# Issuing the page loads of both caches from GpSimd's queue instead of SyncE's, in a two-layer hybrid decoder step

## The reference

```python
# 8 decode sequences, 512 past positions in 4 pages of 128; page_table (8, 4) int32
k_past = cache_k[page_table, j].reshape(bs, n_pages * PAGE_SIZE, DIFF_HEADS, DIFF_HEAD_DIM)
v_past = cache_v[page_table, j].reshape(bs, n_pages * PAGE_SIZE, DIFF_HEADS, DIFF_HEAD_DIM)
...
a = probs(qf[..., :DIFF_HALF], k1) - lam * probs(qf[..., DIFF_HALF:], k2)   # softmax(q k * scale + bias)
o = jnp.einsum('bhqk,bkhd->bqhd', a, vf)
...
mixed = jnp.concatenate([y_pool, o.reshape(B, T, DIFF_WIDTH)], axis=-1)     # pooling groups beside the heads
return mixed @ w_out
```

## Time and profile before

| | |
|---|---|
| Time, median of 3 runs | 1458.28 us (1456.0 to 1458.72) |
| The profiled execution, its own time | 1461.25 us |
| Its span | 1459.5 us, mean granted TensorE clock 0.984 |
| PE busy (matmul) | 1392.3 us, 95% |
| DVE, ACT, POOL busy | 47%, 34%, 25% |
| DMA | 140.92 MB, queue q1 busy for 27.4% of 16 engines' span |
| Page loads | 32 of cache_k and 32 of cache_v, 256 KB each, all by SP |

### The profile page before, as it was taken

The page is one execution under the profiler, slowest core; times in us unless marked ns, Lnnn a source line. Parts: engine busy times, 40 slices in busy tenths (PEclk is TensorE's granted clock), DMA queues, the critical chain, the costliest instruction groups (busy, mean ns, idle before and its releaser), DMA issues.

```text
span 1459.5 us, 28313 instructions
## 1 busy us (share of the span) xinstructions
PE 1392.3 (95%) x11816; PEld 1171.8 (80%) x11816; DVE 685.7 (47%) x979; ACT 499.6 (34%) x711; POOL 371.9 (25%) x465
## 2 busy tenths in 40 slices
PE   8999899999999999899999999998799999999997
PEld 6866588888888888687788788787688888888886
DVE  4556453333333323676676676776443333333222
ACT  5334343322223322334334334334244223223221
POOL 1004312212212001354344344344121212221000
PEclk9999799999999999899999999999999999999999
DMA  6566423422233221100120120120222232233211
GB/s 225 208 215 205 139 87 109 150 97 104 86 125 120 80 108 57 58 30 30 60 86 30 60 86 30 59 88 15 95 94 88 87 115 86 97 115 119 99 61 59
DMA packets 32045, 140.92 MB, mean 97 GB/s; under 512 B 4537, under 2 KB 6841, under 8 KB 20058
## 3 DMA queue, kind: packets, MB, share of 16 engines
q1 hardware_dynamic: 31962, 139.75, 27.4%
HBM read 128.63 MB, written 11.11 MB: 96 GB/s over the span
## 4 chain that ended last, share of the span: by engine, by line
PE 84%; DVE 10%; issue 3%; SPq 1%; DMA 1%; ACT 1%; POOL 0%; DVEq 0%; ACTq 0%; POOLq 0%
PE P L1591 59%; PE P L1963 8%; PE P L1954 7%; DVE arena L1360 2%; PE P L1969 2%; DVE arena L1401 1%; PE P L2151 1%; DVE arena L1515 1%; PE P L2128 1%; PE P L2118 1%; PE P L1805 1%; SPq L338 1%; PE P L2089 1%; PE P L1938 1%; DVE arena L1336 1%
## 5 line engine op out<-in xcount | busy, mean ns | idle before, releaser
L1591 PE MATMUL P<-zh,wh 128*128 128x260 f16 x1728 | 332.8, 274 | 2.3 <-DVE wl L1093 2.1
L1591 PE MATMUL P<-zl,wh 128*128 128x260 f16 x1728 | 332.8, 274 | 0.0
L1591 PE MATMUL P<-zh,wl 128*128 128x260 f16 x1728 | 332.8, 274 | 0.0
L1073 DVE SCALAR_TENSOR_TENSOR wl<-stage,wh 128x2048 f16<-128x2048 f32 (+1 forms) x76 | 187.3, 2465 | 210.2 <-ACT wh L702 196.0
L1591 PE MATMUL P<-arena,wh 128*128 128x260 f16 x1832 | 280.4, 275 | 3.3 <-DVE arena L1336 2.8
L1591 PEld LDWEIGHTS P<-arena,wh 128*128 128x128 f16 x1832 | 178.0, 97 | 32.5 <-issue 4.2
L1591 PEld LDWEIGHTS P<-zh,wh 128*128 128x128 f16 x1728 | 165.8, 97 | 35.1 <-issue 6.5
L1591 PEld LDWEIGHTS P<-zh,wl 128*128 128x128 f16 x1728 | 167.4, 97 | 26.5
L1591 PEld LDWEIGHTS P<-zl,wh 128*128 128x128 f16 x1728 | 167.2, 97 | 26.2
L1591 PE MATMUL P<-arena,wl 128*128 128x260 f16 x916 | 176.9, 274 | 0.0
L702 ACT ACTIVATE wh<-stage 128x2048 f16<-128x2048 f32 (+1 forms) x82 | 165.6, 2020 | 2.8 <-PE P L1954 2.8
(11 more groups left out here) (324 smaller groups left out, 1578.5 us busy)
## 6 DMA issues: line engine op xcount, KB each, us to landing
stage<-w_gu SPq DMA_DIRECT2D x44, 1024.0 KB, 4.8
stage<-w_in SPq DMA_DIRECT2D x23, 1024.0 KB, 4.9
stage<-w_dn SPq DMA_DIRECT2D x16, 1408.0 KB, 5.8
arena<-cache_k SPq DMA_DIRECT2D x32, 256.0 KB, 3.6
stage<-w_out SPq DMA_DIRECT2D x8, 1024.0 KB, 5.1
arena<-cache_v SPq DMA_DIRECT2D x32, 256.0 KB, 3.0
arena<-delta_state SPq DMA_DIRECT2D x8, 512.0 KB, 3.6
o_ds<-arena SPq DMA_DIRECT2D x8, 512.0 KB, 6.7
```

The source lines that it names most:

```text
L1073: nc.vector.scalar_tensor_tensor(out=wl[:, j, 0:words], in0=stage[:, j, 0:words], scalar=WS, in1=wh[:, j, 0:words], op0=MUL, op1=SUB).then ...
L1591: mm = nc.tensor.matmul(pm[j][:, c, :], w[:, wslot, o:o + 128], x[:, k, c * CH:(c + 1) * CH], start=(k == first and w is wh and x is xh), ...
```

## The change

`load_kv` is moved from SP's program to POOL's, with its waits. Nothing is changed in what a load reads or writes, in the number of slots, or in the program of PE, DVE and ACT. In POOL's program the loads get these places: 0 to 2 before the clearing of `qpad` and `apad`, 3 to 10 behind it and ahead of pooling group 0, 11 and 12 behind group 0, and 13 to 15 behind group 1. SP keeps the weights, the bias and the outputs.

```diff
@@ SP: every load_kv call goes, and the function with them
-            load_kv(0)
             project_in(3)
 ...
-            load_kv(1)
             sp.wait_ge(strip_out, 16)
 ...
-            load_kv(2)
             for u in range(4, 8):
                 project_in(u)
-            for n in range(3, 7):
-                load_kv(n)
             project_mix(0)
-            for n in range(7, 11):
-                load_kv(n)
             sp.wait_ge(pm_free, 12)
 ...
             project_mix(1)
-            for n in range(11, 2 * NDEC):
-                load_kv(n)
             sp.wait_ge(dext, 4)
@@ POOL
+            def load_kv(n):
+
+                src, b, s = (cache_k, n, n % NKV) if n < NDEC else (cache_v, n - NDEC, n % NKV)
+                if n >= NKV:
+                    pool.wait_ge(kv_used, n - NKV + 1)
+                for g in range(NPG):
+                    i = b * NPG + g
+                    page = pool.value_load(pt[0:1, i:i + 1], min_val=0, max_val=cache_k.shape[0] - 1)
+                    nc.gpsimd.dma_start(kv[:, s, g, :], src[bass.ds(page, 1)].rearrange("a p n -> (a p) n")
+                                 ).then_inc(kv_in[s], 16)
+
+            pool.wait_ge(c_in, 16 * 7)
+            for n in range(NKV):
+                load_kv(n)
             pool.wait_ge(strip_out, 16)
-            pool.wait_ge(c_in, 16 * 7)
             link(nc.gpsimd.memset(qpad, 0.0))
 ...
             pool.nop().then_inc(consts, 1)
+
+            for n in range(NKV, NDEC + NKV):
+                load_kv(n)
 
             for i, g in enumerate(GROUPS):
 ...
                 nc.gpsimd.tensor_tensor(dT[:, SEQ:T], dT[:, SEQ:T], ext[:, g, :, 15], SUB).then_inc(d_ready, 1)
+                for n in ((11, 12), (13, 14, 15), (), ())[i]:
+                    load_kv(n)
```

More of the change, by code:

```diff
@@ L329, in stream @@
                         weights(src, base + 2 * i + j, j, bass.ds(2 * i + j, 1), words)
[L331 to L340, removed]
             def project_in(u):
```

## The result

| | before | after |
|---|---|---|
| Median (5 runs each) | 1458.28 us (1454.53 to 1459.28) | 1467.18 us (1465.13 to 1469.0) |
| Ratio, 95% interval | | 1.0067 [1.005, 1.0085] |
| The profiled execution, its own time | 1461.25 us | 1466.75 us |
| Its span, mean granted clock | 1459.5 us, 0.984 | 1465.1 us, 0.984 |

The forecast was 1468.4. So the traces say where the time went, and the medians how much it is.

A forecast was written before the change was run, and what follows sets the result against it. PE's weight products, untouched, were taken as the bound (59% of the chain). POOL's line releases the fourth projection at 160.9 + 16p = 181.4 against 171.25, 10.1 us later: 1458.3 + 10.1 = 1468.4 us, range 1460 to 1486.

The forecast's parts named there:

- p = 1.28: Assumed cost in us of one page load on POOL, halfway between 1.10 and 1.45.
- The one line on POOL: Loads 12 to 15 and groups 1 to 3 run in order on POOL, delaying PE's fourth pooling projection by 10.1 us.
- The page: Issuing a page on POOL costs 1.28 us, register work plus DMA instruction, with ends of 0.96 and 2.05.
- DVE beside POOL: Delaying group 0 loosens its collision with DVE; up to 2.5 and some 2 us back, counted as nothing.
- Load 3: On POOL it no longer stands behind SP's eighth weight unit, so PE's full 1.1 us wait is won.
- PE's stalls: PE waits for cache_v at three products, then for POOL at the third and fourth projection, inside the 10.1 us.
- The dear page: Rival, chance 0.27: POOL's DMA instruction costs 0.8 to 1.3 us and POOL bounds the mixer; 25 us late at p = 1.75.
- the second ceiling: POOL's 52 pages and four groups from 76.3 us end at 105.2 + 52p, binding only above p = 1.55.
- Loads in time: Rival, chance 0.09: POOL issues loads 13 to 15 by 157 us, PE doesn't stop; about 10 us faster, 1448.
- The cheap page: Rival, chance 0.09: register work overlaps the DMA before it, a page is 0.76 us or less; no change, 1456 to 1461.
- The rules of the Trainium skill: POOL's DMAs land some 0.4 us later (1468.8); DVE locking POOL out of descriptor writing adds 2 us (1470.4).
- I add no clock cost: Behind the fourth projection PE ran at the low clock in before too, so no clock term was added.

The follow-up runs named there:

- e1: The changed kernel with loads 13 to 15 moved ahead of pooling group 1 on POOL: 1467.29 us, 1.0057 of before.
- e2: The changed kernel with loads 13 to 15 back on SP, loads 0 to 12 staying on POOL: 1454.07 us, 0.9965 of before.
- e3: The changed kernel with loads 11 to 15 back on SP, loads 0 to 10 staying on POOL: 1453.91 us, 0.9968 of before.
- e8: The kernel before with only loads 11 to 15 moved to POOL, loads 0 to 10 staying on SP: 1469.93 us, 1.009 of before.
- e4: The kernel before with pooling group 0 on POOL also waiting for DVE's decode_probs: 1456.47 us, 0.9979 of before.
- e7: The changed kernel with page numbers fixed in the program instead of read from the table: 1465.86 us, 1.005 of before.
- e11: The changed kernel with fixed page numbers and pooling group 0 also waiting for decode_probs: 1462.18 us, 1.003 of before.

## Why the prediction came out right, step by step

The sign and the mechanism held. That the size came so near (8.9 against 10.1) is partly luck: against the trace of before, from which the sum was made, the step is 6.1 us, and 3.0 of the 8.9 come from that execution having been slower than its kernel's median. With the times of after's trace against the steps at p = 1.28:

| step | forecast | measured |
|---|---|---|
| end of the second value product | 140.3 | 137.0 |
| load 12, 4 pages | 5.1 | 5.2 |
| group 1 | 8.8 | 9.3 |
| loads 13 to 15, 12 pages | 15.4 | 13.9 |
| group 2 | 5.3 | 4.9 |
| group 3 | 6.5 | 7.0 |
| fourth projection released | 181.4 | 177.3 |

- **The one line on POOL** (right). Every step of it stands in the trace in the order forecast. e1 shows that the order within it doesn't matter, e2 and e3 that taking loads out of it turns the loss into a gain, e8 that loads 11 to 15 in it are the whole cost: +11.9 us alone.
- **The page** (right, a little large). 1.15 us, where 1.28 was taken between bounds of 0.96 and 2.05; on 16 pages 2.1 us. Of these 0.7 came back, nearly all at load 12, which took 5.2 for 4 pages: its first DMA starts 1.25 us behind the release, 0.1 more than a page, and the last one's 0.54 have no next page to lie beside. The working had added 0.76 of register work and 0.52 of the DMA instruction on POOL; the trace has 0.65 and a gap of 0.50 in the sequencer, while the instruction's 0.54 lies beside the next page. The sum was near for reasons that were partly wrong.
- **DVE beside POOL** (the term that was mis-sized). It said "I leave it at nothing"; the second value product came 4.4 us sooner, of which load 3 explains 0.4, so the relief gave 4.0: all of PE's wait for ACT and the low clock behind it. e4 has it alone: 4.0 us on v-a, and 2.5 in the medians, since a part goes to other waits there. The whole difference between the sum and the trace is then: 10.1 + 0.7 (load 3) - 4.0 (relief) - 1.4 (16 pages, 19.1 for 20.5) + 0.6 (groups, 21.2 for 20.6) = 6.0.
- **Load 3** (right in kind, the gain too large by 0.7). Counted as 1.1 won; 0.4 was. The first page's DMA runs at 77.48, 1.2 us after its release, and the last took 5.71 us to land rather than 3.6.
- **PE's stalls** (wrong in form). Forecast were waits for cache_v at three products and for POOL at the third and fourth projection. There is one of 11.2 us at load 13, whose pages landed 6.4 to 7.6 us after their issue and not the 3.0 of the sum; behind it PE, at 1.2 GHz, was slower than the pages, and reached the third projection only at 170.82, 0.5 us after POOL's release. Only the fourth waited (3.6). The sum doesn't depend on it: the last release is POOL's either way.
- **The rivals.** The dear page falls by 1.15, the second ceiling too (POOL waits for PE's release ahead of load 12, 3.52 us between two pages). Loads in time falls: the last page of load 15 goes out at 164.89, not before 157. The cheap page falls as a price, and e7 shows more: even at 0.53 us a page it would not have been "no change", since group 0 then starts early again and the landing takes over. The slope of 16 us for each us of p holds only while POOL's line ends last.
- **The rules of the Trainium skill.** For a DMA from GpSimd (DMA: Bandwidth & Descriptors, SWDGE vs HWDGE vs iDMA) the trace agrees as far as medians over all pages can tell: landings of 4.0 and 3.5 us against 3.6 and 3.0, 0.4 to 0.5 more. It moved no end, since POOL's line and no landing released the fourth projection. That VectorE in a mode with both ports holds descriptor work back (SBUF — State Buffer, Who interferes with whom) wasn't seen: the DMA instructions at 118.96, 120.11 and 121.25 took 0.54 us each while DVE was busy for 3.89 of 4 us. Whether DVE was in that mode isn't in the trace, and beside most of loads 13 to 15 it stood idle, so this tests the rule weakly. The 2 us worked out from it didn't come: the 12 pages took 13.9 us, 0.1 more than 12 times 1.15.

What stays open: the medians differ by 8.9 and the profile pair by 5.5 (e8: 11.9 and 7.0, from the same trace of before). The records show with what this goes, though not where it lies. The kernel before was executed 86 more times beside the experiments (one outlier of 3633 us aside), and its time follows its mean granted clock: 1454.5 us on average at 0.991, 1457.6 at 0.988, 1462.2 at 0.984. Its profiled execution has 0.984, which only 10 of the 86 are at or under; after's five have 0.983 to 0.985. At 0.984 after's three average 1467.2, 5.0 above the 1462.2, as in the profile pair. So the other 3 to 4 us are executions in which before keeps a clock that after never had. The prediction's "I add no clock cost" was read from an execution of before that had itself lost much clock, so this term was put at nothing on a weak ground. It isn't shown to be a cost of its own, as the clock is also at 0.50 while PE stands idle, which lowers the mean.

## What to carry to other kernels

An engine that computes and also issues loads is one line in order: add its pages and its arithmetic behind the last thing it waits for, and compare the end of that sum with who needs it. The price of an issue was nearly the same on both engines (1.15 and 1.10 us); what cost 9 to 12 us was what stands behind it. And ask what a delayed instruction no longer collides with: holding one group of POOL back by some 4 us won 2.5 us in the kernel before (e4) and 3.3 in e7 (e11). Ask also what the relieved queue now sends earlier: SP's weight unit left 8.5 us sooner than in before, into the landing of the pages.

## What the runs showed of the hardware

- A page load from POOL costs its sequencer 0.50 us beyond the register work, once its operands are ready, while the instruction's 0.54 us on the engine overlap what comes next. With a fixed address 12 of them took 6.41 us.
- From the release to the first DMA instruction of a row it is 1.25 us, both at load 3 and at load 12: the register work and the 0.50 us of its own page, and 0.1.
- The 64 pages are 5120 packets in POOL's queue.
- Three loads issued in 6.4 us had PE waiting for two of them (e7); issued 1.15 us a page, the second and third came in time for a PE at 1.2 GHz.
- A page of 256 KB took 3.1 to 7.6 us to land within one row of twelve on POOL, the longer times beside a 1 MB weight unit of SP and a DMA share of 0.94 to 0.97.
- After a wait of PE of the same 2.5 us the granted clock fell to 0.51 in one execution (before) and stayed at 1.00 in another (e8).
- DVE's copy of 128x8 took 1.24 us beside a sum on POOL and 0.17 without one, so a small instruction on a chain can cost seven times its price.
